# Stick-breaking attention: Softplus on ScalarE replaced by Abs, Exp and Ln, with a maximum and an add on VectorE

## The reference, cut to what matters

```python
def stick_breaking_attention(q, k, v):
    # A[t,s] = sigmoid(z_ts) * prod_{s<j<t} (1 - sigmoid(z_tj)), s < t, in log space
    ...
        valid = kpos[None, :] < (start + jnp.arange(Q_BLOCK))[:, None]
        z = jnp.einsum('bhqd,bhkd->bhqk', a, k, preferred_element_type=jnp.float32)
        log_fail = jnp.where(valid, jax.nn.log_sigmoid(-z), 0.0)
        after = lax.cumsum(log_fail, axis=3, reverse=True) - log_fail
        wts = jnp.where(valid, jnp.exp(jax.nn.log_sigmoid(z) + after), 0.0)
        return jnp.einsum('bhqk,bhkd->bhqd', wts, v, preferred_element_type=jnp.float32)
```

## Time and profile before

| what | value |
|---|---|
| median of 3 runs | 3805.17 us (3803.59 to 3810.74) |
| profiled execution, its own time | 3805.17 us |
| its span in the trace | 3803.4 us |
| PE busy | 3420.3 us (90% of the span) |
| DVE busy | 1492.6 us (39%) |
| ACT busy | 1054.0 us (28%) |
| granted TensorE clock, mean | 0.95 of full speed |

### The profile page before, as it was taken

The page is one execution under the profiler, slowest core; times in us unless marked ns, Lnnn a source line. Parts: engine busy times, 40 slices in busy tenths (PEclk is TensorE's granted clock), DMA queues, the critical chain, the costliest instruction groups (busy, mean ns, idle before and its releaser), DMA issues. The chain is left out here.

```text
span 3803.4 us, 54244 instructions
## 1 busy us (share of the span) xinstructions
PE 3420.3 (90%) x24004; PEld 2571.7 (68%) x24004; DVE 1492.6 (39%) x2149; ACT 1054.0 (28%) x1691; POOL 168.2 (4%) x167
## 2 busy tenths in 40 slices
PE   6989778886988886999998989999999998889999
PEld 5857667754533334887786568877887786567877
DVE  3355656456111115333425443334333424543333
ACT  3225433221000002222324532223222323542222
POOL 0011222131000000000000000000000000000000
PEclk8999889997999998999999999999999999999999
DMA  6140000121799994322211032222222211032321
GB/s 236 45 152 1 3 3 3 33 103 45 306 421 421 421 421 156 106 89 89 89 61 56 1 100 89 90 105 94 89 89 101 99 61 56 1 98 69 111 89 39
DMA packets 173990, 441.09 MB, mean 116 GB/s; under 512 B 5954, under 2 KB 97852, under 8 KB 149180
## 3 DMA queue, kind: packets, MB, share of 16 engines
q1 hardware_dynamic: 173756, 437.61, 31.0%
HBM read 435.49 MB, written 2.10 MB: 115 GB/s over the span
## 5 line engine op out<-in xcount | busy, mean ns | idle before, releaser
L333 PE MATMUL banks<-mix_r,ring_r 128*128 128x512 f32 x1776 | 700.9, 395 | 0.0
L333 PE MATMUL banks<-mix_r,ffn_r 128*128 128x512 f32 x1664 | 665.3, 400 | 10.5 <-ACT mix_r L2438 7.8
L333 PE MATMUL banks<-h_r,ffn_r 128*128 128x512 f32 x1664 | 651.1, 391 | 0.0
L295 DVE TENSOR_TENSOR ring_r<-ring,ffn_r 128x2048 fp32r<-128x2048 f32 (+2 forms) x168 | 357.4, 2127 | 231.1 <-ACT ffn_r L292 231.1
L292 ACT ACTIVATE ffn_r<-ring 128x2048 fp32r<-128x2048 f32 (+2 forms) x168 | 299.6, 1783 | 480.7 <-PE banks L333 474.2
L333 PEld LDWEIGHTS banks<-mix_r,ring_r 128*128 128x128 f32 x1776 | 335.5, 189 | 83.3
L333 PEld LDWEIGHTS banks<-mix_r,ffn_r 128*128 128x128 f32 x1664 | 314.7, 189 | 79.6 <-issue 12.8
L333 PEld LDWEIGHTS banks<-h_r,ffn_r 128*128 128x128 f32 x1664 | 314.8, 189 | 73.4
L2748 PE MATMUL banks<-ring_r,ffn_r 128*128 128x512 f32 x704 | 279.3, 397 | 0.0
L2177 PE MATMUL banks<-ring,arena 128*64 128x512 f32 x1056 | 239.6, 608 | 34.9 <-DMA ring<-in_exp_w_down 20.9
L2747 PE MATMUL banks<-ffn_r 128*128 128x512 f32 x640 | 250.7, 392 | 4.7 <-DVE arena L2698 4.7
(11 more groups left out here) (432 smaller groups left out, 5032.2 us busy)
## 6 DMA issues: line engine op xcount, KB each, us to landing
ring<-in_exp_w_down SPq DMA_DIRECT2D x30, 2048.0 KB, 17.9
ring<-in_w_ffn_gate SPq DMA_DIRECT2D x44, 1024.0 KB, 5.5
ring<-in_w_ffn_up SPq DMA_DIRECT2D x44, 1024.0 KB, 8.0
ring<-in_w_ffn_down SPq DMA_DIRECT2D x20, 2048.0 KB, 7.7
ring<-in_exp_w_gate SPq DMA_DIRECT2D x18, 2048.0 KB, 18.1
ring<-in_exp_w_up SPq DMA_DIRECT2D x18, 2048.0 KB, 17.6
ring<-in_w_in SPq DMA_DIRECT2D x17, 2048.0 KB, 8.2
arena<-in_exp_w_gate SPq DMA_DIRECT2D x14, 2048.0 KB, 18.1
```

Of the source, the lines that this page charges most:

```text
L295: l.did(V.tensor_tensor(lo, x_, hi, ALU.subtract).then_inc(l.sem, 1), name, "lo", v)
L333: ins = TE.matmul(m[1](bank), m[2], m[3], start=m[4], stop=m[5])
```

## The change

Softplus(z) is computed as max(z, 0) + ln(1 + exp(-|z|)). On ACT the three Softplus pieces become three Abs pieces from PSUM, then Exp with scale -1 over the 1280 columns in place, then Ln with bias 1.0 over the 1280 columns in place, each behind a wait for the engine's own last instruction. On DVE three operations are added ahead of the first mask: each reads a piece of z in PSUM, takes the maximum with 0 and adds what ACT left in `sp`. They read banks 0 to 2, which PE may write again only after key `sp`, as before. Nothing changes on PE, in the DMAs or in any other stage.

```diff
@@ st_act
                                 for b, o in full3(0):
                                     n = b.shape[1]
-                                    l.did(S.activation(sp[:, i % 2, o:o + n], b, ACT.Softplus).then_inc(l.sem, 1))
-                                l.name_last(nb, "ln", i)
+                                    l.did(S.activation(sp[:, i % 2, o:o + n], b, ACT.Abs).then_inc(l.sem, 1))
+                                l.wait_ge(*l.own())
+                                l.did(S.activation(sp[:, i % 2, :], sp[:, i % 2, :], ACT.Exp, scale=-1.0).then_inc(l.sem, 1))
+                                l.wait_ge(*l.own())
+                                l.did(S.activation(sp[:, i % 2, :], sp[:, i % 2, :], ACT.Ln, bias=1.0).then_inc(l.sem, 1), nb, "ln", i)
@@ st_dve
                             if i < 6:
                                 l.wait_ge(*past(nb, "ln", i))
+                                for b, o in full3(0):
+                                    n = b.shape[1]
+                                    l.did(V.scalar_tensor_tensor(out=sp[:, i % 2, o:o + n], in0=b, scalar=0.0, in1=sp[:, i % 2, o:o + n],
+                                                                 op0=ALU.max, op1=ALU.add).then_inc(l.sem, 1))
+                                l.wait_ge(*l.own())
                                 mask(sp[:, i % 2, :])
                                 l.name_last(nb, "sp", i)
```

## The result

The changed kernel took 3829.69 us (median of 4 runs, 3821.87 to 3833.84) against 3804.38 us for the kernel before in the same rounds (executions of both kernels, taken in one series): a ratio of 1.0068, with an interval of 1.005 to 1.0087. It is slower, as forecast, but by 25 us where 17 were forecast, and 3829.7 lies above the range of 3814 to 3828. Two further series of the same kernel gave 1.0059 (1.0038 to 1.008) and 1.0052 (1.0032 to 1.0071). The mean of the three is 1.0060, or 22.7 us. The medians of these two series, 3827.52 and 3827.71 us, lie just inside the range, so the miss is one of a few us. Two executions in later rounds, one of the kernel before (4692.93 us) and one of e5 (4426.73 us), ran at a mean granted clock of 0.68 and 0.73 and stand in no ratio.

What follows compares the result with a forecast made beforehand. PE was taken to bound the full rounds and to wait in the opening. Per layer 4.3 + 2.0 + 2.1 + 0.1 = 8.5 us, 17.0 for both: 3805.2 + 17.0 = 3822.2 us, range 3814 to 3828.

Steps and rivals of the forecast that it cites:

- where it waits: Stage of each layer: PE bounds full rounds with 1.6 us to spare; in the opening it waits for the chain.
- the pieces of the chain: Head 0, from z made to masks done: Abs, Exp, load, Ln, load, DVE pieces and masks sum to 7.92 us, against 3.58.
- The 0.1 us at the end of the stage: Round 6, without a z: zc of head 5 waits from 11.96 till about 12.1 us, 0.1 us a layer.
- the clock falls: Behind PE's 6.2 us pause, z of head 1 runs at 1.2 GHz, adding 2.0 us a layer (bounds 0 and 2.1).
- slowed it would still end before sp of head 1 is there: Opening: zc of head 0, some 7.3 us on PE, stays hidden behind head 1's chain even at the slow clock.
- What follows the stage waits behind its fence, so nothing takes this back: Behind each layer's stage: nothing recovers the 8.5 us a layer, 17.0 for both.
- rival E: Later pauses: slow clock behind six of them shortens by 3 us each, giving back 9 us; 3802 at the least; 2%.
- theory 3: From the follow-up runs: stage length shifts later pauses against clock falls; 1074 to 1078 us between stages, or 1072.7 where lengths fit.
- A, the clock holds: Opening: z of head 1 runs at 2.4 GHz, a layer loses 6.5 us, time 3818.2; 18%.
- B, one set: Chain on ACT: Ln and Exp share one table set, no load between; 6 to 9 us in all, 3811 to 3814; 5%.
- C, a load for Abs: Each head's chain: Abs needs a table load and Exp another, 8 us more in a layer, 3838; 3%.
- D, a switch dearer than its load: Head 1's two further table switches cost 1.28 us more each, 2.6 us more in a layer, 3827; 1%.

Runs made afterwards that it cites:

- e5: Changed kernel with Exp in place of Ln in each head's chain, so no table load stands there (result not softplus): ratio 1.0033.
- e3: Kernel before with only heads 2 to 5 of each layer in the new form, heads 0 and 1 keeping Softplus: ratio 0.9998.
- e2: Kernel before with only heads 0 and 1 of each layer in the new form, heads 2 to 5 keeping Softplus: ratio 1.0051.
- e7: Changed kernel run again as it is, a third time: ratio 1.0052.
- e12 to e15: Kernel before with two or four matmuls more in round 4 of each stage, two traces each: stage 86.99 us with two, 88.71 or 88.72 with four.
- e16: Kernel before with three matmuls more in round 4 of each stage: stages 87.86 and 87.85 us, 1072.8 us between them.
- e17: Second trace of the kernel before with three matmuls more in round 4 of each stage: stages 87.85 us, 1075.9 us between them.
- e10: Changed kernel as it is, one more trace: stages 93.12 and 93.19 us, 1074.1 us between them.
- e8: Changed kernel with six unread matmuls on PE ahead of z of head 1 and two ahead of z of head 2: ratio 1.0043.
- e4: Changed kernel with five unread matmuls on PE ahead of z of head 1: ratio 1.0047, stage 93.64 us in both layers.

## Why the prediction was wrong

**Right: where it waits.** PE bounds the full rounds, and the opening is where the chain is bare. e3 (84.34 us) and e2 (93.2 us) show both halves of this.

**Right: the pieces of the chain.** 7.83 us for head 0 against 7.92 forecast; z of head 1 came 4.25 us later (4.3 forecast), the chain of head 1 at full clock costs 1.96 us (2.1). The bias of Ln costs nothing; I had put it too high by 0.09 us. The 0.1 us at the end of the stage isn't there: zc of head 5 starts 11.97 us behind z of head 5. Abs brought no load, Ln did.

**Right that the clock falls, by 0.6 us too low in its price.** I gave 2.0 us; it is 2.6. z of head 1 by itself is 2.2 us late (ACT begins 4.67 us behind its start, and not 2.46). The other 0.4 us is the step "slowed it would still end before sp of head 1 is there": PE came to z of head 2 only at 2153.21, when the masks had been done since 2152.75. The sum behind that step doesn't carry it. 4.4 us for z and 7.3 x 1.87 for zc make 18, against 13.7 for the chain, so it held only if the clock came back in time, and it came back too late for that. In the one stage where it came back sooner, layer 1 of e7, PE waited for 0.89 us ahead of z of head 2, as forecast, and the stage took 92.52 us. The stages together cost 17.4 us where 17.0 were forecast.

**Wrong: "What follows the stage waits behind its fence, so nothing takes this back", with the later clock falls put at nothing.** This is the term that failed. I had six long pauses behind the first stage, each with a fall of the clock, and let what follows them go either way, with the mean of the one trace I had. In the sum the term is 0; in four traces of the changed kernel the parts behind the stages took 5.3 us more in the mean than in three of the kernel before (4.0 between them, 1.3 behind the second). In the part between, the clock stood at 1.2 GHz for 57.1 us in the mean where it had stood there for 48.0, so 4.0 us of time came with 9.1 us more at the low clock. That some four tenths of it is time fits the half that I had reckoned in rival E, with the other sign. The three traces of the kernel before lie at the cheapest end of all twenty; my starting point was a cheap case and no mean one, as far as the traces tell.

How lasting this is stays open. e12 to e15 took 4.6 to 8.7 us more over both parts with nothing but a longer stage, and e16 returned to the old values at a length at which theory 3 had expected that. But e17, the same program, did so in one part of two, e10 took 1074.1 us, and e3 took 6.6 us more with a stage of the old length and no cost in the rounds. So neither the length of the stage nor the change's work on ACT and DVE is shown to be the cause. What is shown is that the later clock falls took up to 6 us more between the stages, and that the forecast gave them nothing. The rest of the distance from 22.7 us to the 25.3 of the first series is within its interval of 19 to 33 us.

**The rivals.** A, the clock holds: it would need filled pauses, as in e8. B, one set: the trace has the loads; e5 prices it at 1.0033, or 12.6 us, where I had 6 to 9. The clock falls in its pause as well, and z of head 1 and zc of head 0, both slowed, then set the pace: from z of head 1 to z of head 2 it takes 12.98 us instead of 9.66, where I had the chain hidden. C, a load for Abs: absent. D, a switch dearer than its load: absent, 0.02 us around each load again. E, faster: in these traces the later falls went the other way.

## What to carry to other kernels

In a software-pipelined loop the price of a longer chain is paid where the pipeline fills; count the chain against the cover of each round, and the opening rounds by themselves. A pause on PE costs more than its length when it brings the clock down, here 2.6 us on top of 6.2 in each layer. Matmuls that filled it took the fall away only when they filled the next pause too. And where many executions of one program differ by more than the change is worth, compare the durations of a stage between fixed instructions, and let the rounds, not a single pair of spans, judge the rest of the program.

## What the runs showed of the hardware that I had not expected

In these traces the length of a short pause doesn't tell whether the clock falls. Behind the 1.83 us before z of head 1 in the kernel before, z ran at clock 1.00. In e4 the clock fell 1.1 us behind the end of a pause of 1.89 us, which followed one of 1.80; the stage of layer 1 took the same 93.64 us. Filling one pause moved the fall to the next.

The time of a stretch that no edit touches goes with how long the clock stays low in it: between the stages 1072.6 us with 47.9 us at 1.2 GHz, 1078.9 with 60.7. Two traces of one program can differ in this, by 3.8 us in the changed kernel (e10 and the first) and by 3.1 us with three matmuls more (e16 and e17). What decides it stays open.
